# Sparse attention of a two-block model on one core: meta keys of eight heads put in one key block, and a gate chunk moved from the rope stage into the attention steps

## What is computed

```python
for l in range(DEPTH_2):
    proj = jnp.einsum('bld,de->ble', h, w_in[l])
    a, g, zc, q, k, v, za, qi, ki, wi = jnp.split(proj, IN_SPLITS, axis=-1)
    y_conv = conformer_conv_branch(a, g, zc, conv_w[l], conv_b[l], conv_ln_g[l], conv_ln_b[l])
    ...                                            # rope on q, k, qi, ki
    y_attn = dsa_sparse_attention(q, k, v, qi, ki, wi, topk) * jax.nn.silu(za)
    y = jnp.einsum('ble,ed->bld', jnp.concatenate([y_conv, y_attn], axis=-1), w_out[l])
    h = layer_norm(DEEPNORM_ALPHA * h + y, post_ln_g[l], post_ln_b[l])

# within dsa_sparse_attention, per block of queries; idx: the 68 best keys by the indexer's score
s = jnp.einsum('bqhd,bqkhd->bqhk', qb, kg).astype(jnp.float32) * (HEAD_DIM ** -0.5)
s = jnp.where(valid[:, :, None, :], s, -jnp.inf)
p = jax.nn.softmax(s, axis=-1).astype(v.dtype)
return jnp.einsum('bqhk,bqkhd->bqhd', p, vg)
```

## Time and profile before

| | us |
|---|---|
| median of 3 runs | 884.41 |
| lowest and highest | 884.2, 887.57 |
| profiled execution, whole | 884.17 |
| its span in the trace | 882.3 |
| busy in it: PE, DVE, ACT, POOL | 860.6, 497.7, 506.4, 627.5 |

### The profile page before, as it was taken

How to read it: one execution, slowest core, us unless ns; L and a number is a source line. 1 busy time by engine, 2 the same in 40 slices (tenths; PEclk the granted TensorE clock), 3 DMA queues, 4 the chain that set the end, 5 groups by cost and what they waited for, 6 DMA issues and landing times.

```text
span 882.3 us, 17095 instructions
## 1 busy us (share of the span) xinstructions
PE 860.6 (98%) x6763; PEld 830.4 (94%) x6763; DVE 497.7 (56%) x1111; ACT 506.4 (57%) x1027; POOL 627.5 (71%) x384
## 2 busy tenths in 40 slices
PE   9999999999999999999999999999989999998996
PEld 7988999999998998999999999999979999998886
DVE  4413111699837947654332003888965559888664
ACT  5537655722346557544444445555878566568773
POOL 5823755555556987999998889986884869867353
PEclk9999999999999999999999999999999999999998
DMA  9625534342432465455554675664411527644201
GB/s 288 201 80 182 184 97 144 103 137 96 137 103 97 157 225 192 140 194 193 189 162 145 187 209 136 195 193 143 144 49 49 156 66 235 191 134 156 97 1 48
DMA packets 140894, 128.68 MB, mean 146 GB/s; under 512 B 12784, under 2 KB 138608, under 8 KB 140688
## 3 DMA queue, kind: packets, MB, share of 16 engines
q1 hardware_dynamic: 140304, 126.80, 46.5%
q10 hardware_dynamic: 512, 0.79, 0.3%
HBM read 126.40 MB, written 1.05 MB: 144 GB/s over the span
## 4 chain that ended last, share of the span: by engine, by line
PE 86%; ACT 6%; DVE 5%; issue 2%; POOL 1%; POOLq 0%; DVEq 0%; ACTq 0%
PE PS L652 22%; PE PS L654 21%; PE PS L653 21%; PE PS L935 3%; PE PS L643 2%; PE PS L1140 1%; PE PS L700 1%; PE PS L696 1%; PE PS L697 1%; PE PS L1084 1%; PE PS L1111 1%; PE PS L897 1%; PE PS L760 1%; ACT w_hi L1413 1%; POOL x_lo L1262 1%
## 5 line engine op out<-in xcount | busy, mean ns | idle before, releaser
L1251 POOL TENSOR_TENSOR w_lo<-ring,w_hi 128x1024 fp32r<-128x1024 f32 (+3 forms) x261 | 549.2, 2122 | 183.0 <-ACT w_hi L1413 172.6
L652 PE MATMUL PS<-x_hi,w_hi 128*128 128x256 f32 (+1 forms) x1442 | 420.2, 291 | 3.3 <-ACT zoneB L1396 1.7
L654 PE MATMUL PS<-x_hi,w_lo 128*128 128x256 f32 (+1 forms) x1442 | 409.6, 284 | 0.0
L653 PE MATMUL PS<-x_lo,w_hi 128*128 128x256 f32 (+1 forms) x1442 | 409.1, 284 | 0.0
L1413 ACT ACTIVATE w_hi<-ring 128x1024 fp32r<-128x1024 f32 (+3 forms) x259 | 240.6, 941 | 74.3 <-PE PS L654 65.9
L652 PEld LDWEIGHTS PS<-x_hi,w_hi 128*128 128x128 f32 x1442 | 272.2, 189 | 6.7 <-issue 3.6
L653 PEld LDWEIGHTS PS<-x_lo,w_hi 128*128 128x128 f32 x1442 | 271.6, 188 | 0.7 <-issue 0.2
L654 PEld LDWEIGHTS PS<-x_hi,w_lo 128*128 128x128 f32 x1442 | 272.0, 189 | 0.0
L2258 DVE SCALAR_TENSOR_TENSOR PS<-zoneA,cols,PS 128x256 f32<-128x256 f32 x240 | 98.4, 482 | 0.2
L1396 ACT ACTIVATE zoneA<-PS 128x272 f32<-128x272 f32 (+2 forms) x68 | 26.1, 384 | 99.8 <-PE PS L654 99.7
L1396 ACT ACTIVATE zoneB<-PS 128x256 f32<-128x256 f32 (+4 forms) x115 | 40.7, 376 | 57.8 <-DVE PS L2225 37.6
(11 more groups left out here) (340 smaller groups left out, 1359.6 us busy)
## 6 DMA issues: line engine op xcount, KB each, us to landing
ring<-in_w_in SPq DMA_DIRECT2D x58, 1024.0 KB, 5.4
ring<-in_w_ffn_in SPq DMA_DIRECT2D x22, 1024.0 KB, 5.1
ring<-in_w_out SPq DMA_DIRECT2D x12, 1024.0 KB, 5.2
ring<-in_w_ffn_out SPq DMA_DIRECT2D x16, 704.0 KB, 4.6
ring<-in_w_mla_o SPq DMA_DIRECT2D x4, 1024.0 KB, 5.3
ring<-in_w_hg_o SPq DMA_DIRECT2D x4, 1024.0 KB, 5.1
ring<-in_w_kv_b SPq DMA_DIRECT2D x2, 1024.0 KB, 5.4
ring<-in_w_q_b SPq DMA_DIRECT2D x2, 768.0 KB, 4.8
```

Source lines behind the costliest of these rows:

```text
L652: mm(out_, hi_w, hi_x, start=start, stop=False)
L653: mm(out_, hi_w, lo_x, start=False, stop=False)
L654: return mm(out_, lo_w, hi_x, start=False, stop=stop)
L1251: ins = sub(lo_w, src, hi_w, ALU.subtract)
```

## The change

The 16 meta keys of a query tile no longer share a key block with other keys of the same head. Key blocks now start behind the meta keys, so tile 0 has one block of 128 and tile 1 two. The meta keys of all eight heads are gathered into one block of 8 x 16 = 128 rows: ACT copies their probabilities into `meta_keys` after the last head's Exp (steps 7 and 15), PE transposes this once, and one product, 512 columns wide, adds it to all heads in bank 6. For it the third block of `v2` holds the meta values as a block diagonal, built by two ACT copies into `v_blocks` at ROPE_FILL's third chunk. `at2_p` keeps all eight heads of a tile. The meta queries of layer 0 use the same block: DVE spreads the probabilities of step 16 over it with a mask in a new constant. POOL's zeroing of pads goes, and one of `v_blocks` comes.

The chunk za1 leaves the rope stage; its eight k-steps are dealt out over steps 0 to 7, and ACT takes it, and rounds the piece that hangs on it, at step 7. In layer 1 the k-steps of za2 that stood at steps 0 and 1 and from 9 on now stand at steps 8 to 13. In layer 0 the three filler matmuls of steps 0 and 1 (line 756) go. Layer 0's copies of the meta queries (`meta_q`) move from the rope stage to steps 4 to 7. Banks 0 and 1 are exchanged for the chunks from a1 to qi0 where before they were for those behind; of all pairs of neighbours that alters one, a1, which now follows g0 in its bank and no longer g1. In layer 1 POOL makes the low part of `wo0`'s second piece after its first two sums, not before.

```diff
-ROPE_FILL = [("v", 2), ("v", 3), ("zc", 0), ("zc", 1), ("zc", 2), ("zc", 3), ("za", 0), ("za", 1)]
+ROPE_FILL = [("v", 2), ("v", 3), ("zc", 0), ("zc", 1), ("zc", 2), ("zc", 3), ("za", 0)]
...
-    spread = {s_: [("za", 2, s_ - 8, s_ - 7)] for s_ in range(8, 16)} if l == 0 else \
-        {0: [("za", 2, 0, 2)], 1: [("za", 2, 2, 3)], **{s_: [("za", 2, s_ - 6, s_ - 5)] for s_ in range(9, 14)}}
+    spread = {s_: [("za", 1, s_, s_ + 1)] for s_ in range(8)}
+    spread |= {s_: [("za", 2, s_ - 8, s_ - 7)] for s_ in range(8, 16)} if l == 0 else \
+        {**{s_: [("za", 2, s_ - 8, s_ - 7)] for s_ in range(8, 12)}, 12: [("za", 2, 4, 6)], 13: [("za", 2, 6, 8)]}
...
-    _g = CHUNK[f"L{_l}kw", 1]
-    for _p in range(_g, CHUNK[f"L{_l}wo3", 1] + 1):
+    for _p in range(CHUNK[part(f"L{_l}a", 1)], CHUNK[f"L{_l}kw", 1]):
         BANK[_p] = (_p + 1) % 2
...
-        at2_s, at2_p, at2_pt = z(2, L), z(DSA_LAG + 1, 3 * P), z(2, 3 * P)
+        at2_s, at2_p, at2_pt = z(2, L), z(HEADS, L), z(2, 3 * P)
+        block_p = at2_p[:, 0, META:META + P]
...
-        vT2 = keep[:, 0:4 * L].rearrange("p (c t) -> p c t", c=4)
+        z = Zone(keep)
+        vT2, v_blocks, meta_keys = z(4, L), z(4, P), z(P)
...
-            return t, h, (2 + t) * P, (META, META + P, 0)[t], (META + P, L, META)[t]
+            return t, h, (1 + t) * P, (META, META + P, 0)[t], (META + P, L, META)[t]
+
+        def last_head(i):
+
+            return i < DSA_TILES and i % HEADS == HEADS - 1
...
-                        t0, n = KEY_CHUNKS[TURN_AT[i]]
-                        g = CHUNK[f"{T}vt", TURN_AT[i]]
+                        x = TURN_AT[i]
+                        g = CHUNK[f"{T}vt", x]
                         bank_free(g)
                         out_of_psum(pe, *part(f"{T}v", 3))
+                        if x == 2:
+                            pe.wait_ge(sem("v_blocks"), 2 * (l + 1))
                         for c in range(4):
-                            last = nc.tensor.transpose(PS[0:n, BANK[g], c * P:(c + 1) * P], vT2[:, c, t0:t0 + n], ident)
+                            last = nc.tensor.transpose(PS[:, BANK[g], c * P:(c + 1) * P],
+                                                       vT2[:, c, META + x * P:META + (x + 1) * P] if x < 2 else v_blocks[:, c, :],
+                                                       ident)
                         done(last)
...
-                        p, b = at2_p[:, j % (DSA_LAG + 1), :], PS[:, 4 + j % 2, :]
+                        p, b = at2_p[:, j % HEADS, :], PS[:, 4 + j % 2, :]
                         if j < DSA_TILES:
                             for k0 in range(0, width, P):
-                                last = nc.tensor.transpose(b[:, k0:k0 + P], p[:, k0:k0 + P], ident)
+                                last = nc.tensor.transpose(b[:, k0:k0 + P], p[:, META + k0:META + k0 + P], ident)
+                            if last_head(j):
+                                pe.wait_ge(sem("meta_keys"), 2 * l + t + 1)
+                                last = nc.tensor.transpose(b[:, width:width + P], meta_keys, ident)
                         else:
-                            last = nc.tensor.transpose(b[0:META, 0:P], p[:, 0:META], ident)
+                            last = nc.tensor.transpose(b[:, 0:P], block_p, ident)
                         last.then_inc(sem(f"{A}_pt"), 1)
...
                         for k0 in range(0, width, P):
                             last = mm(PS[:, 6, h * HD:(h + 1) * HD], at2_pt[:, j % 2, k0:k0 + P],
-                                      v2[:, k0 // P, h * HD:(h + 1) * HD], start=(k0 == 0), stop=(k0 == width - P))
+                                      v2[:, k0 // P, h * HD:(h + 1) * HD], start=(h == 0 and k0 == 0), stop=False)
+                        if last_head(j):
+                            last = mm(PS[:, 6, :], at2_pt[:, j % 2, width:width + P], v2[:, 2, :], start=False, stop=True)
                         last.then_inc(sem(f"{A}_o"), 1)
...
-                bank_free(CHUNK[part(f"{T}za", 2)])
-                    if l == 0 and s < 2:
-                        turns_over(2 - s, BANK[CHUNK[part(f"{T}za", 2)]])
...
-                            r = slice(h % 2 * HD, h % 2 * HD + HD)
-                            mm(PS[r, TURN_BANKS[c], 0:META], v2[0:META, 0, h * HD:(h + 1) * HD],
-                               meta_pt[0:META, h * META:(h + 1) * META], start=True, stop=True)
+                            mm(PS[:, TURN_BANKS[c], 0:META], v2[:, 2, c * P:(c + 1) * P],
+                               meta_pt[:, h * META:(h + 1) * META], start=(h % 2 == 0), stop=(h % 2 == 1))
...
-            nc.gpsimd.memset(at2_p[:, :, L:3 * P], 0.0)
+            nc.gpsimd.memset(v_blocks[:, :, :], 0.0)
...
-                    nc.gpsimd.memset(kir[:, :, :], 0.0)
-                    nc.gpsimd.memset(v2[:, 2, :], 0.0)
-                nc.gpsimd.memset(at2_p[:, :, META + P:2 * P], 0.0).then_inc(sem("pads"), 1)
+                    nc.gpsimd.memset(kir[:, :, :], 0.0).then_inc(sem("pads"), 1)
...
-                if l:
-                    lo_piece(SPLIT[f"{T}wo0", 1])
                 added_chunks(l, q_from)
-                if l == 0:
-                    lo_piece(SPLIT[f"{T}wo0", 1])
+                lo_piece(SPLIT[f"{T}wo0", 1])
...
+                    if i == 2:
+                        out_of_psum(act, *part(f"{T}v", 3))
+                        for half in range(2):
+                            r = slice(64 * half, 64 * half + 64)
+                            blocks = v_blocks[r, 0:1, half * META:half * META + META]
+                            blocks = bass.AP(tensor=blocks.tensor, offset=blocks.offset,
+                                             ap=[blocks.ap[0], [P + 2 * META, 4], [1, META]])
+                            af(blocks, vT2[r, :, 0:META], ACT.Copy).then_inc(sem("v_blocks"), 1)
                     if i in TURN_AT:
-                        rows = KEY_CHUNKS[TURN_AT[i]][1]
-                        take(f"{T}vt", TURN_AT[i], v2[0:rows, TURN_AT[i], :], rows=rows, n=512)
+                        take(f"{T}vt", TURN_AT[i], v2[:, TURN_AT[i], :], n=512)
                     if i < 6:
                         beside_q(i + 2)
                     if i == 6:
                         warm(ACT.Exp)
                         part_heads(0)
-                    if i == 7:
                         part_heads(1)
-                    if i >= 4 and l == 0:
-                        act.wait_ge(sem("q_roped"), i - 3)
-                        for h in (2 * (i - 4), 2 * (i - 4) + 1):
-                            af(meta_q[:, h // 2, h * META:(h + 1) * META], q2r[:, h // 2, 0:META], ACT.Copy,
-                               scale=head_rows[h % 2]).then_inc(sem("meta_q"), 1)
+
+                def part_meta(m):
+
+                    act.wait_ge(sem("q_roped"), m + 1)
+                    for h in (2 * m, 2 * m + 1):
+                        af(meta_q[:, h // 2, h * META:(h + 1) * META], q2r[:, h // 2, 0:META], ACT.Copy,
+                           scale=head_rows[h % 2]).then_inc(sem("meta_q"), 1)
+
                 def dsa_attention(i):
 
                     A = f"{T}att"
                     j = i - DSA_LAG
                     if 0 <= j < DSA_N[l]:
-                        width = dsa_step(j)[2]
+                        width = dsa_step(j)[2] + last_head(j) * P
                         act.wait_ge(sem(f"{A}_pt"), j + 1)
...
-                        if i > DSA_LAG:
-                            act.wait_ge(sem(f"{A}_pt"), i - DSA_LAG)
-                        af(at2_p[:, i % (DSA_LAG + 1), 0:nk], at2_s[:, i % 2, 0:nk], ACT.Exp, scale=-1.0,
+                        if i >= HEADS:
+                            act.wait_ge(sem(f"{A}_pt"), i - HEADS + 1)
+                            if i % HEADS == 0:
+                                act.wait_ge(sem("meta_keys"), 2 * l + i // HEADS)
+                        af(at2_p[:, i % HEADS, 0:nk], at2_s[:, i % 2, 0:nk], ACT.Exp, scale=-1.0,
                            bias=at2_min[:, i:i + 1], accum_out=at2_sum[:, i:i + 1]).then_inc(sem(f"{A}_exp"), 1)
+                        if last_head(i):
+                            act.wait_ge(sem(f"{A}_exp"), i + 1)
+                            af(meta_keys.rearrange("p (h k) -> p h k", h=HEADS), at2_p[:, :, 0:META], ACT.Copy)\
+                                .then_inc(sem("meta_keys"), 1)
 
                 for s in range(DSA_N[l] + DSA_LAG + 1):
                     dsa_attention(s)
                     if s < 2:
                         part_heads(2 + s)
+                    if l == 0 and 4 <= s < 8:
+                        part_meta(s - 4)
...
-                            p = at2_p[:, last % (DSA_LAG + 1), 0:META]
+                            p = at2_p[:, 0, 0:META].rearrange("p (o k) -> p o k", o=1).to_broadcast([P, HEADS, META])
+                            heads = cst("head_block").rearrange("p (h o) -> p h o", o=1).to_broadcast([P, HEADS, META])
```

(5 more changed lines are left out.)

12 lines of the change are left out of this document (6 added, 6 removed).

## The result

| | us |
|---|---|
| changed kernel, median of 6 | 890.36 (889.46 to 893.73) |
| before, median of 6 | 885.0 (883.28 to 887.57) |
| ratio | 1.0066, 95% interval 1.0043 to 1.0089 |
| profiled execution, whole and span | 893.73 and 891.9 |

A forecast was written before the change was run, and what follows sets the result against it. PE carried 86% of the span, but ACT's queue at step 7 was taken to decide. 884.17 + 2.7 (layer 0) + 2.6 (layer 1) - 0.9 (banks) = 888.6; forecast 888.5 us, range 884.5 to 891.8.

The forecast's parts named there:

- Matmuls removed at the entry: Ahead of the first scores: taking za1's matmuls away leaves PE a 3.9 us hole and saves 0.
- ACT's queue at step 7: Between Exp 7 and the copy PE awaits: 2.1 us more work, copy +1.1, PE idle some 2.5 in step 9.
- First mean: Layer 0, after the late copy and the wide product: PE's first mean comes 1.2 us later.
- rival C: Step 9's idle PE is a second hole; half clock behind it costs 1.3 to 1.7 us per layer: 891.3, chance 0.21.
- Between the means: Chain over DVE, ACT and POOL from first to second mean: keeps its length, 7.7 to 8 us; the delay shrinks by 0.1.
- Layer 0's end: Behind the second mean: `meta_keys` copy +0.5, wide product +0.66, lighter steps -0.4, dearer output turning +0.8, meta probabilities -0.4.
- The turning: Layer 0, turning the output with 128 x 128 weights: four blocks get dearer, +0.8 us taken.
- The meta probabilities: Layer 0's end, DVE's new operation in place of one of 1.58 us: -1.3 to 0, -0.4 taken.
- Layer 1, +2.6: Layer 1's stage: mean +2.0, `meta_keys` +0.5, wide product less lighter steps +0.3, 0.5 swallowed, clock +0.3.
- Banks, -0.9: Chunk a1 no longer waits 0.31 us for g1's take nor loses 0.16 on weights: -0.47 per layer.
- Rival A: Attention stages bound by PE, so saved matmuls and filled idle time pay in full: 874.2, chance 0.08.
- Rival B: ACT's queue absorbed, the copy late by 1 us less, each layer ending 1 to 2 us earlier: 885, chance 0.18.

The follow-up runs named there:

- e3: Changed kernel with ACT's take of za1 and the rounding behind it moved from step 7 to step 10; ratio to the kernel before 1.0012.
- e1: The changed kernel measured once more, unaltered, as a control; ratio to the kernel before 1.0075.
- e8: Changed kernel with za1's dealing-out undone and layer 0's za2 finished at step 13, not 15; ratio to the kernel before 0.9987.
- e2: Kernel before, with only banks 0 and 1 exchanged for the chunks from a1 to qi0; ratio 0.9998.
- e7: Kernel before, with only the dealing-out of za1 and what goes with it, without the meta block; ratio 1.0045.
- e9: Changed kernel with 8 small filler matmuls ahead of step 9's transpose in both layers; ratio to the kernel before 1.0041.
- e10: Changed kernel with the take of za1 at step 10 and 8 filler matmuls ahead of the first scores; ratio to the kernel before 0.9989.

## Why the prediction was right, point by point

- **Matmuls removed at the entry: 0.** Right: the hole is 3.86 and 3.85 us (3.9 said), and from `wo` of layer 0 to the first scores of layer 1 it took 133.45 us, 133.30 before.
- **Exp 7, -1.0.** It came 10.99 us behind the first scores, 12.34 before: -1.35.
- **ACT's queue at step 7, +2.1.** The copy's distance from Exp 7 grew by 1.96. So the copy came 13.84 us behind the first scores, 13.23 before: +0.6 where I had +1.1, and PE idled 1.95 for my 2.5. e3 shows this queue to be the largest part of the loss.
- **First mean, +1.2.** +2.5 and, in e1, +2.9. The step that failed is the clock's: I had the stretch at the hole (it came, from 643.5, and in e1 from 641), and put the second one into rival C at 1.3 to 1.7 us. With the late take alone the mean came at +16.39, +0.2.
- **Between the means.** 7.55 and, in e1, 7.85 us (7.88 before) for the 7.7 to 8 said, and PE waited 0.90 for POOL's sums at the second, where it had waited for nothing. So the chain is a little shorter than PE's work was before, and the lighter steps gained 0.3 where I had 0.1.
- **Layer 0's end, +1.2 by my terms (0.5 + 0.66 - 0.4 + 0.8 - 0.4).** From the second mean to `wo` 12.86 us before, 13.71 in e1: +0.85. Two terms were mis-sized and nearly cancel (-0.6 and +0.8), which was luck; with both put right the terms give 1.4, and no term of mine explains the 0.5 down to 0.85. The turning costs 0.2 and not 0.8: four small products took 0.51 us (0.29 in the earlier trace rows), the whole of it 2.39 and not 2.19. The meta probabilities cost +0.4 and not -0.4: PE's wait for them grew from 0.41 before to 0.85 in e1 (rows below). The upper bound that I gave, no gain, was the nearer end, and even that excluded the loss. That the two block each other the Trainium skill's page "SBUF — State Buffer" ("Who interferes with whom") had right, and e8's 0.35 against 1.78 us bears it out.

```profile
675.24 0.28 PE L1131 MATMUL PS<-const,zoneB 128*16 128x128 f32 x1 [0.41 <-DVE zoneB L2396]
```

```profile
676.58 0.33 PE L1145 MATMUL PS<-const,zoneB 128*128 128x128 f32 x1 [0.85 <-DVE zoneB L2421]
```

- **Layer 1, +2.6.** The mean came 14.80 us behind the first scores before; it is +4.45 in the first profile and +2.44 in e1 (+2.0 said); behind the second mean nothing was lost (10.50 and 10.49 us, 10.54 before), where I had +0.3.
- **Banks, -0.9.** By e2's trace layer 0 gained 0.4 and layer 1, where POOL's low part came next (0.20 in the changed kernel), 0.1. I had looked at what a1 waited for, and in layer 1 not at what would be late next.
- **POOL's order.** As said it costs nothing; e7 shows the wait that the old order brings, 1.55 us at layer 1's first mean.
- **The sum.** 888.5 said, 890.36 measured: within the range, but over the 888.8 above which I gave 0.43, against 0.48 for no change to speak of. The truth lies between my forecast and rival C (891.3): C's condition, two falls in a layer, was met in three of the four stages profiled, and its price was about right, since e3 takes away the stall and its low clock together for 4.8 to 5.6 us, of which the stalls' own length explains 1.2 in each layer; the rest, 2.4 to 3.2 us, is C's 2.8, and e9, which fills the stall alone, gives 2.2 to 3.0. The page that I drew on for C speaks of longer gaps than step 9's, so "by that rule both holes of a layer cost" was my reading of it and not what it says. The stages of the changed kernel differ by 1.5 and 2.6 us between its two profiles, so that single terms fit within 1 us is in part luck. Rival A (874.2) is out, but not only by the queue, as I had said: e10 has neither queue nor low clock in its stages and is still only 0.1% faster than before, with stages of 36.98 and 32.65 us (36.93 and 33.02). PE's saved matmuls don't show in them; in layer 0 PE waits for ACT (0.66 and 0.71 us), POOL (0.91) and DVE (0.85) instead. Rival B (885, the queue absorbed) is out by the time and by PE's 1.95 and 1.54 us idle in step 9, though the copy did come 0.5 us earlier than I reckoned, half of B's condition.

## What to carry to other kernels

Work that is moved into another engine's idle time takes its followers along: here PE had room for the k-steps, but the take and the rounding that hang on them went to ACT's fullest step, and PE waited for those. Before a chunk is taken out of a place, ask what the engine does there instead; if it is nothing, the steps behind may run at half clock, as they did here behind 3.86 us, and filler matmuls that end before the awaited data can cost less than the hole (8 of them, 2.0 us in e10). Time a filler from a row of its own kind, and count its records: 14 for 8 turned 2.0 us of gain into a loss.
